# GpSimd instead of VectorE for the combination of the middle token tile's expert rows

## The chip, the cores and the metric

The kernel runs on one core of one Trainium2 chip. The metric is the device time of one execution in microseconds, the median over several runs. Times inside an execution are counted from the start of the profile's span.

## The reference, cut to what matters

One inference step of a two-layer backbone over 384 tokens of 1024 columns: 128 context tokens and 256 latent tokens. Each layer is a token mixer (HGRN2 in layer 0, a Fourier mixer in layer 1) and a hierarchical mixture of experts (16 experts, two chosen for a token), each with a gated residual; one norm closes the whole. The part at issue is the end of the mixture and what reads it:

```python
hid = jax.nn.silu(jnp.einsum('td,edf->tef', t, w_gate)) * jnp.einsum('td,edf->tef', t, w_up)
y = jnp.einsum('tef,te,efd->td', hid, gates.astype(hid.dtype), w_down)
...
x = x + g2[:, None, :] * _hier_moe(h, ...)      # end of a layer
...
h = _modulate(_rmsnorm(x, w['norm1_g'][i]), sh1, sc1)   # start of the next
...
return _rmsnorm(x, w['final_norm_g']), states
```

So for each token x + g2 * (w1 * y1 + w2 * y2) is wanted, where y1 and y2 are the rows that its two experts gave, w1 and w2 its weights and g2 the gate vector of its group.

## The kernel before, in words

All values are fp32. The tokens lie in three tiles of 128 (tile 0 is the context, tiles 1 and 2 the latent tokens), each a 128x1024 part of the tensor `x` in SBUF. The experts run as a loop (TensorE L755 for gate and up, L772 for down), their output rows are scattered to a buffer in HBM by GpSimd (L1340), and weights stream through a ring of six slots from SyncE's queue (`moe_units`, L334 to L349).

When the last rows of a layer are out, GpSimd sets `all_out`, and SyncE's `expert_rows` (L351 to L357) loads the rows back, one DMA for each tile, into `yall[:, t, 0]` and `yall[:, t, 1]`, the first and second expert's rows of the tile's tokens. Behind these it asks for the tables of the Fourier mixer and the next weights. Then

- ScalarE's `combine` (L932) multiplies the second rows of each tile by their weight in place (L937) and signals `second`;
- VectorE's `combine` (L1242) takes the tiles in order 0, 1, 2, three operations each, every one waiting for the one before: first rows times weight plus second rows (L1249), times the gate (L1251), added to x (L1252, signals `x_done`);
- ScalarE's `squares` (L814, the operation at L823) sums the squares of each tile, in order of the tiles, as its `x_done` comes;
- GpSimd's `rms` turns each sum into the factor 1/sqrt by two instructions on one column (L1410, L1413);
- after layer 0 VectorE's `normalise` (L992, the operation at L995) multiplies each tile by its factor, `columns` (L1001) prepares two vectors, and TensorE turns the tiles (L476): tiles 0 and 1 first, tile 2 behind. ScalarE (L831) and VectorE (L1016) bring the result back modulated, and TensorE begins the Fourier mixer (L658);
- after layer 1 VectorE's last loop (L1325) multiplies each tile by its factor and the final gain, and SyncE stores it (L424).

In every queue the order is that of the program text. On GpSimd, `rms("a1")` and `rms("fin")` stand right behind `experts(0)` and `experts(1)`. Between the two combinations lie the Fourier mixer, its output projection, the router (`route`) and layer 1's experts. The first six weight loads of layer 1 (L340) wait for a product of the modulation or of the projection, the later ones (L346, L349) for the experts' own progress.

Other lines that are named below: L1336, L1337 and L1346 are GpSimd's memsets at the start of its `experts`; L400 to L406 are the loads of the Fourier tables and weights, L332 those of the modulation's weights.

Of the kernel before, what the change touches and what calls it, by code (L numbers as in the profile page):

```python
# [25 lines left out]
ALU = mybir.AluOpType  # L26
# [5 lines left out]
TT = 3  # L32
# [40 lines left out]
def program(nc, io, scratch):  # L73
    with ExitStack() as ctx:
        def sb(name, shape, dt=F32):
            return ctx.enter_context(nc.sbuf_tensor(name, shape, dt))

        def sem(name):
            return ctx.enter_context(nc.semaphore(name))
# [3 lines left out]
        x = sb("x", [P, TT, D])  # L83
        hT = sb("hT", [P, KD, T])
        gate_bc = sb("gate_bc", [P, 2, 2, D])
# [11 lines left out]
        def c_(name):  # L97
            at, tile = (FIRST_AT, first) if name in FIRST_AT else (CONST_AT, const)
            a, b = at[name]
            return tile[:, a:b]  # L100
# [62 lines left out]
        yall = work[:, 0:2 * TT * D].rearrange("p (t c n) -> p t c n", t=TT, c=2)  # L163
# [5 lines left out]
        hid = me.take(F // 2).rearrange("p (j f) -> p j f", j=2)  # L169
        hidT = me.take(F // 2).rearrange("p (j s) -> p j s", j=2)  # L170
# [23 lines left out]
        wgt = sb("wgt", [P, 2, TT])  # L194
# [12 lines left out]
        gates_in = [sem(f"gates_in{i}") for i in range(4)]  # L207
# [27 lines left out]
        M = []  # L235
        for l in range(2):
            M.append({n: sem(f"moe{l}_{n}") for n in [
                "logits_t", "logits_sb", "logits", "chosen", "pos_mm", "onehots", "idx_mm", "idx_ready", "back_mm", "back_act",
                "hrow_out", "zeroed", "si_set", "gi_set", "gathered", "turned", "xt_sb", "gate_up_mm",
                "silu", "hid", "hid_turned", "hidT", "y_mm", "y_sb", "scattered", "gate_up_used", "used", "all_out", "second", "weights", "x_done",  # L240
                "exp_in", "exp_out"]})
        yback = [sem(f"expert_rows_in{t}") for t in range(TT)]
        chain = sem("dve_chain")
# [567 lines left out]
        def _(act):  # L811
            A = nc.scalar.activation

            def squares(name):  # L814

                for t in range(TT):
                    if name == "a0":
                        act.wait_ge(x_ready, 1)
                    elif name in ("m0", "m1"):
                        act.wait_ge(out_x[int(name[1])], 4 + t)  # L820
                    else:
                        act.wait_ge(M[0 if name == "a1" else 1]["x_done"], t + 1)
                    A(xn_of(name)[:, t, :], x[:, t, :], ACT.Square, accum_out=stat[:, t:t + 1]).then_inc(n_sq, 1)  # L823

            def modulate(name, l, which):
# [156 lines left out]
        def _(dve):  # L982
# [3 lines left out]
            def step(ins):  # L986

                count[0] += 1
                ins.then_inc(chain, 1)
                dve.wait_ge(chain, count[0])  # L990

            def normalise(name, tiles=range(TT)):  # L992
                for t in tiles:
                    dve.wait_ge(n_rs, 3 * NORM[name] + t + 1)
                    V.tensor_scalar(xn_of(name)[:, t, :], x[:, t, :], stat[:, 3 + t:4 + t], None, ALU.mult  # L995
                                    ).then_inc(n_xn, 1)
# [245 lines left out]
            def combine(l):  # L1242

                m = M[l]
                for t in range(TT):
                    dve.wait_ge(yback[t], 16 * (l + 1))
                    dve.wait_ge(m["second"], t + 1)
                    a, b = yall[:, t, 0, :], yall[:, t, 1, :]
                    step(V.scalar_tensor_tensor(out=a, in0=a, scalar=wgt[:, 0, t:t + 1], in1=b,  # L1249
                                                op0=ALU.mult, op1=ALU.add))  # L1250
                    step(V.tensor_tensor(a, a, gate_bc[:, 1, GROUP_OF[t], :], ALU.mult))  # L1251
                    V.tensor_tensor(x[:, t, :], x[:, t, :], a, ALU.add).then_inc(m["x_done"], 1)  # L1252
# [45 lines left out]
            experts(0)  # L1298
            dve.wait_ge(gates_in[1], 16 * 2)
            combine(0)  # L1300
            normalise("a1")
            dve.wait_ge(col_set, 10)
            columns("a1", 1, 0)
# [14 lines left out]
            experts(1)  # L1318
            dve.wait_ge(gates_in[3], 16 * 2)
            combine(1)  # L1320
            dve.wait_ge(M[1]["x_done"], TT)
            dve.wait_ge(fin_in, 16)
            for t in range(TT):
                dve.wait_ge(n_rs, 3 * NORM["fin"] + t + 1)
# [5 lines left out]
        def _(pool):  # L1330
            G_ = nc.gpsimd

            def experts(l):
# [68 lines left out]
                pool.wait_ge(m["xt_sb"], k1)  # L1402
                pool.sem_inc(m["all_out"], 1)

            def rms(name):

                for t in range(TT):
                    n = 3 * NORM[name] + t + 1
                    pool.wait_ge(n_sq, n)
                    G_.tensor_scalar(stat[:, t:t + 1], stat[:, t:t + 1], 1.0 / D, EPS, ALU.mult, ALU.add  # L1410
                                     ).then_inc(n_ms, 1)
                    pool.wait_ge(n_ms, n)
                    G_.tensor_tensor(stat[:, 3 + t:4 + t], stat[:, t:t + 1], c_("minus_half")[:, 0:1], ALU.pow  # L1413
                                     ).then_inc(n_rs, 1)
# [44 lines left out]
            pool.wait_ge(out_x[0], 6)  # L1459
            mod_gates(1, 0, gates_in[2])  # L1460
            experts(0)
            rms("a1")
            for U in (22, 23):
                gate_rows(U)
            rms("m1")
            mod_gates(1, 1, gates_in[3])
            experts(1)
            rms("fin")


# [107 lines left out]
```

## Time and profile before

| | us |
|---|---|
| median of 3 runs | 1196.88 |
| lowest, highest | 1189.55, 1198.07 |
| profiled execution | 1192.05 |
| its span | 1190.0 |
| TensorE busy | 985.6 (83%) |
| VectorE busy | 246.4 (21%) |
| GpSimd busy | 150.5 (13%) |
| mean granted TensorE clock | 0.917 of full speed |

In the profile PE is TensorE's matmul, PEld its weight load, DVE VectorE, ACT ScalarE, POOL GpSimd and SP SyncE; a name with q is the engine's queue. A row of the order of time gives start, length, engine, line, operation, output and inputs, shape and count, and in brackets how long the engine was idle before it and what ended that. The span goes from the first to the last instruction; 2.05 us of the profiled execution lie around it.

### The profile page before, as it was taken

The numbers are of one execution on the slowest core, as the hardware profiler recorded it, in microseconds if no ns is written. First come the engines' busy times: TensorE is split into PE (matmuls) and PEld (weight loads), VectorE is DVE, ScalarE is ACT, GpSimd is POOL, SyncE is SP. The second block draws the span as 40 slices with busy tenths as digits, with TensorE's granted clock in tenths as the row PEclk, the third lists the DMA queues.
The fourth block names the chain that finished last, engine by engine and source line by source line (L and its number), as shares of the span: only waits on it lengthen the run. The fifth ranks groups of instructions, "written<-read, shape, count | busy, mean of one in ns | idle before, by whom it ended". The sixth has DMA issues, their size and how long they took to land.

```text
span 1190.0 us, 21552 instructions
## 1 busy us (share of the span) xinstructions
PE 985.6 (83%) x8838; PEld 572.6 (48%) x8839; DVE 246.4 (21%) x546; ACT 229.0 (19%) x481; POOL 150.5 (13%) x249
## 2 busy tenths in 40 slices
PE   4799976999887895988898998299959998787770
PEld 3466545665456444544454554256445554444430
DVE  1100167100175144000000111500351010000004
ACT  1111102211102022211122222320131221121112
POOL 0000000100000120211111212100022221111112
PEclk9899989999987896988899999699978998998995
DMA  9966410777201741699989894815541999999943
GB/s 390 391 260 232 192 40 2 319 273 283 90 16 60 300 174 63 260 425 427 427 353 428 357 374 190 359 72 212 230 161 34 424 383 426 428 424 427 427 208 159
DMA packets 34184, 318.34 MB, mean 268 GB/s; under 512 B 6788, under 2 KB 9284, under 8 KB 16080
## 3 DMA queue, kind: packets, MB, share of 16 engines
q1 hardware_dynamic: 22016, 293.93, 59.9%
q0 software_dynamic: 8704, 18.33, 4.1%
q10 hardware_dynamic: 3408, 5.24, 1.2%
q8 instruction: 47, 0.77, 0.3%
q14 instruction: 9, 0.07, 0.0%
HBM read 309.12 MB, written 17.33 MB: 274 GB/s over the span
## 4 chain that ended last, share of the span: by engine, by line
PE 64%; DMA 23%; DVE 5%; issue 4%; ACT 2%; SPq 1%; POOLq 0%; POOL 0%; DVEq 0%; ACTq 0%
DMA ring<-in_moe_w_up 17%; PE ps L755 16%; PE ps L508 11%; PE ps L511 7%; PE ps L646 7%; PE ps L772 6%; PE ps L440 3%; DMA ring<-in_w_mod 2%; DMA work<-hrow,gi 2%; PE ps L548 2%; PE ps L658 2%; PE ps L718 1%; PE ps L675 1%; PE ps L487 1%; ACT hT L831 1%
## 5 line engine op out<-in xcount | busy, mean ns | idle before, releaser
L755 PE MATMUL ps<-ring,work 128*64 128x256 f32 x2432 | 304.0, 407 | 54.5 <-DMA ring<-in_moe_w_up 52.5
L755 PEld LDWEIGHTS ps<-ring,work 128*64 128x64 f32 x2432 | 187.4, 147 | 171.5 <-DMA ring<-in_moe_w_up 52.5
L772 PE MATMUL ps<-ring,work 128*64 128x512 f32 x608 | 145.3, 598 | 0.0
L508 PE MATMUL ps<-hT,ring 128*128 128x384 f32 x384 | 129.6, 496 | 5.2 <-ACT hT L831 5.2
L1235 DVE TENSOR_TENSOR work<-work,ps 128x128 f32<-128x128 f32 x76 | 21.8, 287 | 405.7 <-ACT work L924 405.7
L508 PEld LDWEIGHTS ps<-hT,ring 128*128 128x128 f32 x384 | 73.1, 193 | 56.2 <-ACT hT L831 5.3
L511 PE MATMUL ps<-ring,hT 128*128 128x512 f32 x192 | 91.6, 632 | 0.8 <-issue 0.8
L646 PE MATMUL ps<-ring,work 128*128 128x512 f32 x192 | 86.5, 611 | 1.3 <-ACT work L886 0.7
L772 PEld LDWEIGHTS ps<-ring,work 128*64 128x64 f32 x608 | 40.3, 136 | 55.3 <-issue 43.9
L440 PE MATMUL ps<-ring,scond 128*2 128x128 f32 x1536 | 48.0, 278 | 16.2 <-DMA ring<-in_w_mod 16.2
L646 PEld LDWEIGHTS ps<-ring,work 128*128 128x128 f32 x192 | 37.2, 196 | 48.3 <-issue 46.4
L511 PEld LDWEIGHTS ps<-ring,hT 128*128 128x128 f32 x192 | 37.5, 200 | 46.3 <-issue 45.9
L924 ACT ACT_TABLE_LOAD x38 | 48.8, 1283 | 51.4 <-issue 51.3
L1363 POOL COPY gi<-slots_idx 128x1 uint32 (+1 forms) x40 | 7.4, 185 | 392.5 <-issue 330.1
L440 PEld LDWEIGHTS ps<-ring,scond 128*2 128x2 f32 x1536 | 38.8, 86 | 27.9 <-issue 24.4
L926 ACT ACTIVATE work<-ps 128x128 f32<-128x128 f32 x76 | 21.1, 278 | 161.6 <-PE ps L751 97.4
L1340 POOL DMA_INDIRECT yrows<-work,si x44 | 45.1, 1026 | 53.7 <-POOL si L1373 35.1
L924 ACT ACTIVATE work<-ps 128x128 f32<-128x128 f32 x76 | 21.1, 278 | 157.3 <-PE ps L755 157.3
L1366 POOL DMA_INDIRECT work<-hrow,gi x40 | 42.2, 1056 | 33.8 <-POOL gi L1363 30.4
L1421 POOL DMA_DIRECT2D modrow<-mod_row x16 | 9.6, 602 | 277.4 <-DVE mod_row L1031 277.4
L1238 DVE COPY work<-ps 128x512 f32<-128x512 f32 x38 | 26.3, 692 | 70.0 <-PE ps L718 70.0
L929 ACT ACTIVATE work<-ps 128x512 f32<-128x512 f32 x38 | 22.7, 597 | 83.0 <-PE ps L772 70.6
(156 smaller groups left out, 771.3 us busy)
## 6 DMA issues: line engine op xcount, KB each, us to landing
ring<-in_moe_w_gate SPq DMA_DIRECT2D x32, 2048.0 KB, 13.2
ring<-in_moe_w_up SPq DMA_DIRECT2D x32, 2048.0 KB, 17.6
ring<-in_moe_w_down SPq DMA_DIRECT2D x32, 2048.0 KB, 21.7
ring<-in_w_mod SPq DMA_DIRECT2D x24, 2048.0 KB, 10.4
ring<-in_hgrn_w_in SPq DMA_DIRECT2D x10, 2048.0 KB, 11.9
work<-yrows SPq DMA_DIRECT2D x6, 1024.0 KB, 6.9
gate_bc<-modrow POOLq DMA_DIRECT2D x8, 512.0 KB, 6.0
ring<-in_hgrn_w_out SPq DMA_DIRECT2D x2, 2048.0 KB, 7.9
```

The source lines that it names most:

```text
L440: last = mm(ps[32 * c:32 * c + 2, bank, at:at + P], scond[:, :, k], slot3(s)[:, k, c * P:(c + 1) * P], start=(k == 0), stop=(k == KD - 1))
L508: last = mm(bank[:, 0:T], W[:, k, c * P:(c + 1) * P], hT[:, k, :], start=(k == 0), stop=(k == KD - 1))
L511: last = mm(bank, hT[:, k, c * P:(c + 1) * P], W[:, k, :], start=(k == 0), stop=(k == KD - 1))
L548: last = mm(bank[g * SMALL:(g + 1) * SMALL, o:o + SMALL], L[:, a:a + SMALL], R[:, a:a + SMALL], start=(j == 0), stop=(j == len(pairs) - 1))
L646: last = mm(ps[:, n % 4, :], src[:, k, t * P:(t + 1) * P], slot3(s)[:, k, :], start=(k == 0), stop=(k == KD - 1))
L658: last = mm(ps[:, 4 + n % 4, :], hT[:, 2 * g + k, t * P:(t + 1) * P], dft_c[:, k, :], start=(k == 0), stop=(k == 1))
L755: last = mm(ps[h * SLOTS:(h + 1) * SLOTS, GU_BANK[j], 0:2 * P], xt[:, k % 4, k // 4 * SLOTS:(k // 4 + 1) * SLOTS], Wgu[:, :, at:at + P], s ...
L772: last = mm(ps[h * SLOTS:(h + 1) * SLOTS, Y_BANK, :], hidT[:, j, q * SLOTS:(q + 1) * SLOTS], slot_d(S[2])[:, 2 * q + j, h * C512:(h + 1) * ...
L924: A(sg[:, j, :], ps[:, GU_BANK[j], 0:P], ACT.Silu).then_inc(m["silu"], 1)
L1238: V.tensor_copy(xt[:].rearrange("p k s -> p (k s)"), ps[:, XT_BANK, :]).then_inc(m["xt_sb"], 1)
L1340: G_.indirect_dma_start(out=scratch["y"][l], out_offset=bass.IndirectOffsetOnAxis(ap=si[:, 0:1], axis=0), in_=ysb, in_offset=None, bounds_ ...
L1366: G_.indirect_dma_start(out=xg, out_offset=None, in_=scratch["hrow"][l], in_offset=bass.IndirectOffsetOnAxis(ap=gi[:, 0:1], axis=0), bound ...
```

## The change

VectorE's `combine` goes over tiles 0 and 2 alone. A new `combine` on GpSimd, right behind its `experts` and ahead of its `rms`, does tile 1 in four instructions, each waiting for the one before. ScalarE's square of tile 1 waits for GpSimd's signal, and VectorE waits for it before it normalises (layer 0) or begins the final products (layer 1). ScalarE's own multiply of the second rows stays for all three tiles.

```diff
--- before.py
+++ after.py
@@ -237,7 +237,7 @@
             M.append({n: sem(f"moe{l}_{n}") for n in [
                 "logits_t", "logits_sb", "logits", "chosen", "pos_mm", "onehots", "idx_mm", "idx_ready", "back_mm", "back_act",
                 "hrow_out", "zeroed", "si_set", "gi_set", "gathered", "turned", "xt_sb", "gate_up_mm",
-                "silu", "hid", "hid_turned", "hidT", "y_mm", "y_sb", "scattered", "gate_up_used", "used", "all_out", "second", "weights", "x_done",
+                "silu", "hid", "hid_turned", "hidT", "y_mm", "y_sb", "scattered", "gate_up_used", "used", "all_out", "second", "weights", "x_done", "pool_sum", "pool_gated", "pool_x_done",
                 "exp_in", "exp_out"]})
         yback = [sem(f"expert_rows_in{t}") for t in range(TT)]
         chain = sem("dve_chain")
@@ -818,8 +818,10 @@
                         act.wait_ge(x_ready, 1)
                     elif name in ("m0", "m1"):
                         act.wait_ge(out_x[int(name[1])], 4 + t)
+                    elif t == 1:
+                        act.wait_ge(M[0 if name == "a1" else 1]["pool_x_done"], 1)
                     else:
-                        act.wait_ge(M[0 if name == "a1" else 1]["x_done"], t + 1)
+                        act.wait_ge(M[0 if name == "a1" else 1]["x_done"], t // 2 + 1)
                     A(xn_of(name)[:, t, :], x[:, t, :], ACT.Square, accum_out=stat[:, t:t + 1]).then_inc(n_sq, 1)
 
             def modulate(name, l, which):
@@ -1242,7 +1244,7 @@
             def combine(l):
 
                 m = M[l]
-                for t in range(TT):
+                for t in (0, 2):
                     dve.wait_ge(yback[t], 16 * (l + 1))
                     dve.wait_ge(m["second"], t + 1)
                     a, b = yall[:, t, 0, :], yall[:, t, 1, :]
@@ -1298,6 +1300,7 @@
             experts(0)
             dve.wait_ge(gates_in[1], 16 * 2)
             combine(0)
+            dve.wait_ge(M[0]["pool_x_done"], 1)
             normalise("a1")
             dve.wait_ge(col_set, 10)
             columns("a1", 1, 0)
@@ -1318,7 +1321,8 @@
             experts(1)
             dve.wait_ge(gates_in[3], 16 * 2)
             combine(1)
-            dve.wait_ge(M[1]["x_done"], TT)
+            dve.wait_ge(M[1]["x_done"], 2)
+            dve.wait_ge(M[1]["pool_x_done"], 1)
             dve.wait_ge(fin_in, 16)
             for t in range(TT):
                 dve.wait_ge(n_rs, 3 * NORM["fin"] + t + 1)
@@ -1402,6 +1406,22 @@
                 pool.wait_ge(m["xt_sb"], k1)
                 pool.sem_inc(m["all_out"], 1)
 
+            def combine(l):
+
+                m = M[l]
+                a, b = yall[:, 1, 0, :], yall[:, 1, 1, :]
+                pool.wait_ge(m["weights"], 1)
+                pool.wait_ge(yback[1], 16 * (l + 1))
+                G_.tensor_scalar(a, a, wgt[:, 0, 1:2], None, ALU.mult).then_inc(m["pool_sum"], 1)
+                pool.wait_ge(m["second"], 2)
+                pool.wait_ge(m["pool_sum"], 1)
+                G_.tensor_tensor(a, a, b, ALU.add).then_inc(m["pool_sum"], 1)
+                pool.wait_ge(gates_in[1 + 2 * l], 16 * 2)
+                pool.wait_ge(m["pool_sum"], 2)
+                G_.tensor_tensor(a, a, gate_bc[:, 1, 1, :], ALU.mult).then_inc(m["pool_gated"], 1)
+                pool.wait_ge(m["pool_gated"], 1)
+                G_.tensor_tensor(x[:, 1, :], x[:, 1, :], a, ALU.add).then_inc(m["pool_x_done"], 1)
+
             def rms(name):
 
                 for t in range(TT):
@@ -1459,12 +1479,14 @@
             pool.wait_ge(out_x[0], 6)
             mod_gates(1, 0, gates_in[2])
             experts(0)
+            combine(0)
             rms("a1")
             for U in (22, 23):
                 gate_rows(U)
             rms("m1")
             mod_gates(1, 1, gates_in[3])
             experts(1)
+            combine(1)
             rms("fin")
 
 
```

## Rows read from the trace of the kernel before

**Rows 1.** the page's busy table: busy us, share, instructions

```profile
PE 985.6 (83%) x8838; PEld 572.6 (48%) x8839; DVE 246.4 (21%) x546; ACT 229.0 (19%) x481; POOL 150.5 (13%) x249
```

**Rows 2.** the chain of waits, layer 0: start us, us, what

```profile
744.57 4.76 DMA work<-yrows
...
758.15 1.29 DVE work L1249
...
760.72 1.24 DVE x L1252
...
761.98 1.16 ACT work L823 x2
```

**Rows 3.** order of time, all engines, 750 to 765 us

```profile
750.72 1.28 DVE L1249 SCALAR_TENSOR_TENSOR work<-work,wgt 128x1024 f32<-128x1024 f32 x1 [11.35 <-ACT work L937]
751.92 1.15 ACT L937 ACTIVATE work<-work,wgt 128x1024 f32<-128x1024 f32 x1 [1.35 <-DMA work<-yrows]
...
755.02 1.15 ACT L937 ACTIVATE work<-work,wgt 128x1024 f32<-128x1024 f32 x1 [1.95 <-DMA work<-yrows]
...
758.37 1.50 POOL L1413 TENSOR_TENSOR stat<-stat,first 128x1 f32<-128x1 f32 x1
...
761.86 1.57 DVE L995 TENSOR_SCALAR work<-x,stat 128x1024 f32<-128x1024 f32 x2
...
763.58 4.71 PE L476 MATMUL ps<-first,work 128*128 128x128 f32 x24 [23.07 <-DVE work L995]
764.15 0.75 DVE L995 TENSOR_SCALAR work<-x,stat 128x1024 f32<-128x1024 f32 x1 [0.72 <-POOL stat L1413]
```

**Rows 4.** VectorE's three lines: ns min/median/max, starts

```profile
L1249 DVE SCALAR_TENSOR_TENSOR work<-work,wgt x6: 1276/1278/1283, 750.7 to 1173.5; 128x1024 f32<-128x1024 f32 x6
...
L1251 DVE TENSOR_TENSOR work<-work,gate_bc x6: 1224/1224/1226, 752.0 to 1174.8; 128x1024 f32<-128x1024 f32 x6
...
L1252 DVE TENSOR_TENSOR x<-x,work x6: 1224/1225/1226, 753.3 to 1176.1; 128x1024 f32<-128x1024 f32 x6
```

**Rows 5.** order of time, all engines, 1166 to 1181 us

```profile
1166.05 1.28 DVE L1249 SCALAR_TENSOR_TENSOR work<-work,wgt 128x1024 f32<-128x1024 f32 x1 [11.46 <-ACT work L937]
...
1177.31 2.48 DVE L1325 SCALAR_TENSOR_TENSOR work<-x,stat,gate_bc 128x1024 f32<-128x1024 f32 x2
...
1178.55 1.30 POOL L1410 TENSOR_SCALAR stat<-stat 128x1 f32<-128x1 f32 x1 [0.86 <-ACT work L823]
...
1180.51 1.28 DVE L1325 SCALAR_TENSOR_TENSOR work<-x,stat,gate_bc 128x1024 f32<-128x1024 f32 x1 [0.72 <-POOL stat L1413]
```

**Rows 6.** VectorE, then GpSimd, 441 to 443 us

```profile
441.70 1.79 DVE L995 TENSOR_SCALAR work<-x,stat 128x1024 f32<-128x1024 f32 x1
...
441.93 0.54 POOL L1336 MEMSET work<- 128x512 f32 x1
442.39 0.55 POOL L1337 MEMSET work<- 128x512 f32 x1
442.99 0.53 POOL L1346 MEMSET slots_idx<- 128x1 uint32 x1
```

**Rows 7.** GpSimd's two lines of rms: ns min/median/max, starts

```profile
L1410 POOL TENSOR_SCALAR stat<-stat x15: 183/192/1297, 13.9 to 1178.5; 128x1 f32<-128x1 f32 x15
...
L1413 POOL TENSOR_TENSOR stat<-stat,first x15: 550/556/1825, 14.2 to 1179.9; 128x1 f32<-128x1 f32 x15
```

**Rows 8.** SyncE's issues behind the expert rows

```profile
745.89 0.67 SPq L400 DMA_DIRECT2D work<-in_dft_c  x1
...
802.85 0.43 SPq L340 DMA_DIRECT2D ring<-in_moe_w_gate  x1
...
839.01 0.33 SPq L340 DMA_DIRECT2D ring<-in_moe_w_down  x1
```

**Rows 9.** stretches: busy us, PEclk, DMA share, GB/s

```profile
742.08:763.58 21.50, 0.00 (x1) 0.03 (x1) 12.44 (x11) 6.78 (x9) 6.37 (x7) 0.54 0.86 351
...
770.00:775.00 5.00, 4.99 (x12) 2.36 (x13) 0.00 (x0) 1.19 (x2) 0.00 (x0) 1.00 0.24 102
```

## The prediction

> **What bounds the kernel now.** I read the page's busy table first: TensorE is busy 83% of the span and VectorE 21% [rows 1], so VectorE's total is no bound; only its stretches on the chain of waits can cost. The chain of the work that ended last [rows 2] says which these are: behind each layer's expert loop it goes over the load of the expert rows, the three tiles' combination on VectorE (L1249, L1251, L1252), the tile squares on ScalarE and the small root on GpSimd, and TensorE stands still meanwhile (23.07 us, up to 763.58 [rows 3]). The change edits just this stretch, twice: after layer 0, where TensorE waits, and after layer 1, where the end of the program waits.
>
> The order of time in layer 0 is in [rows 3], the length of one VectorE operation in [rows 4]: 1.28, 1.22 and 1.22 us, and all six calls of each within 0.01 us. From 750.72 to 761.95 us VectorE runs the nine almost without a gap (9 operations of 1.24 us are 11.2), so the combination is VectorE-bound, not bound by the loads: tile 1's rows are there at 751.9 (ScalarE's L937 starts on them), tile 2's at 755.0. Layer 1 shows the same, 415.33 us later [rows 5].
>
> **What the change takes away.** Three VectorE operations a layer, 1.28 + 1.22 + 1.22 = 3.7 us. If that were all, tile 2 would be ready some 2 us earlier in layer 0: its second rows come from ScalarE at 755.02 + 1.15 = 756.2 [rows 3], and 3.7 us behind that is 759.9 against 761.95.
>
> **What it adds.** Four GpSimd operations over 128x1024 a layer: a multiply by the weight (one tensor input), and three with two tensor inputs (add, gate, add to x). No row has such an operation. The nearest: GpSimd's memset of 128x512 takes 0.54 us [rows 6], twice that is 1.09 us for one pass over 1024 columns; VectorE's own 1.22 us [rows 4]. The multiply: at least one pass, 1.09; at most two, 2.18 (read, then write). An operation of two inputs: at least one pass, 1.09; at most three, 3.27 (two reads and a write, one behind another). I take 1.09 for the multiply, which the one-input pass is nearest to, and 2.18 for the two-input ones, the two reads one after the other and the write beside them, halfway between the ends.
> The Trainium skill (GPSIMD Engine Reference, Elementwise — side-by-side cycle accounting) gives 4497 ns for an add over 2048 columns; an estimate by that page is 2.25 us for 1024, and the sum would be 0.4 us higher. No run here shows it yet.
>
> **The waits it adds.** GpSimd waits for tile 1's rows (there at 751.9), for ScalarE's weighted second rows (751.92 + 1.15 = 753.07) and for gates that were loaded long before; behind it in GpSimd's order stand the roots, for which VectorE's L995 waits. ScalarE's square of tile 1 waits for GpSimd's last sum, and tile 2's square stands behind it. VectorE waits for that sum ahead of all normalisation, columns and modulation. The renumbered waits of the squares ask for the same tile as before and cost nothing.
>
> **What lies beside what.** The decisive question is whether GpSimd's four run beside VectorE's six. The rows answer for one side. A one-element GpSimd instruction alone takes 0.19 us (L1410) or 0.55 us (L1413) [rows 7]; in the combination L1413 from 758.37 takes 1.50 [rows 3] and ends 0.44 us behind VectorE's L1249 (758.15 + 1.28 [rows 2]); L1410 at 1178.55 takes 1.30 and ends 0.06 us behind the second final product of VectorE (1177.31 + 2.48) [rows 5]. So a VectorE operation with two SBUF inputs holds GpSimd off until it ends. The other side: VectorE's normalisation (L995), 0.75 us in the combination [rows 3], takes 1.79 us beside GpSimd's two memsets, 1.04 more, which is about the two memsets' 1.09; and the one-element memset right behind takes 0.53, until L995 ends [rows 6]. So GpSimd holds VectorE off too, for one kind of operation. That VectorE's two-input operations were never stretched [rows 4] says little, as only one-element GpSimd instructions met them. I take it that they take turns in both directions.
> The Trainium skill (SBUF — State Buffer, SBUF: two separate sides) has a rule that speaks against the change and reaches further than the rows: a VectorE instruction with two SBUF inputs and a GpSimd instruction that reads SBUF exclude each other, the later one waiting until the other is done. By it the sum is the one below; by the unstretched rows alone it would be the third case below.
>
> **Layer 0, step by step.** With turns, VectorE and GpSimd alternate, each always waiting when the other ends: L1249 of tile 0 ends at 752.00 [rows 3]; multiply to 753.09; gate of tile 0 to 754.31; GpSimd's add to 756.49; x of tile 0 to 757.72; GpSimd's gate to 759.90; L1249 of tile 2 to 761.18; GpSimd's add to x to 763.36; gate of tile 2 to 764.58; x of tile 2 to 765.81. That is 3.86 us later than 761.95. In short: 1.09 + 3 x 2.18 = 7.63 added to one shared line, 3.7 removed.
> What is late next: the new work stands ahead of rms in GpSimd's order, and VectorE waits for pool_x_done before it normalises anything. Before, tiles 0 and 1 had their roots while VectorE was still combining, and L995 ran twice from 761.86. Now the root of tile 0 lands 0.45 behind x of tile 2, at 766.26; L995 of tile 0 (0.75) to 767.05; GpSimd's pair for tile 1 (0.19 + 0.55 and gaps, 0.9) to 767.95; L995 to 768.7, where TensorE can begin its turns (763.58 before); the pair for tile 2 to 769.6, where L995 of tile 2 starts, 5.4 us behind its 764.15. ScalarE's squares (1.16 us with their sum [rows 2], tile 1 behind 763.4, tile 2 behind 765.8) lie beside this and end at 767.0, in time for tile 2's pair. If the small pairs slip in beside L995, it is 3.9 instead of 5.4. I take 5.4.
> Nothing covers it. The DFT tables are asked for at 745.9 [rows 8], whatever the combination does, and the later loads (802.85, 839.01) wait for TensorE's own progress, so layer 1's weight stream moves with TensorE and the 5.4 us reach the end. TensorE's granted clock is 0.54 over the standstill and 1.00 from 770 [rows 9]; a standstill 5 us longer gives no reason for another level behind it, and I charge nothing.
>
> **Layer 1.** The same alternation from 1167.33 [rows 5] brings x of tile 2 to 1181.14 and the root of tile 0 to 1181.6. The final products (L1325, 1.28 us) then take turns with GpSimd's pairs: tile 0 to 1182.9, pair 1183.8, tile 1 to 1185.1, pair 1185.9, tile 2 starts at 1185.95, against 1180.51: 5.4 us. With the pairs beside the products it would be 3.7. What follows, the store and the end, is as before.
>
> **Sum.** 5.4 + 5.4 = 10.8 us. The profiled execution took 1192.05 us (span 1190.0), so the like of it would take 1202.9. The median of the runs shown is 4.8 higher, 1196.88, and the runs spread from 1189.55 to 1198.07; as the forecast is for a median I put it on that one: 1207.7 us, 0.9% slower. About 1% is what a measurement of this kernel can tell from no change, 12.0 us; the forecast is just inside.
>
> **The rivals.**
> 1. GpSimd is slower than I take it: three passes for two inputs and two for the multiply, turns as above. Each of four operations is 1.09 longer, twice: +8.7, so +19.5 us, 1216.4, slower by 1.6%. For it: three streams through an engine that shares its way with VectorE; against it: the memsets do a pass in 0.54 per 512. It decides from 2.38 us an operation on (1.2 us missing to 12.0, over six operations).
> 2. VectorE is not held off by GpSimd, while GpSimd still waits for it. VectorE ends at 759.95; GpSimd's multiply to 753.1, add to 755.4, gate to 757.7, and x, held off until gate 2 ends at 758.7, to 760.9. Squares, pairs and L995 then run to about where they did: +0.4 in layer 0, some -0.7 in layer 1: 1196.6. For it: [rows 4]; against it: [rows 6].
> 3. Nobody holds anybody off: GpSimd ends at 760.0, TensorE's wait ends 0.6 earlier, the last product 1.7 earlier: -2.3 us, 1194.6. Against it: [rows 3, 5].
> Even the best of these does not reach 1% faster: the squares and the roots of tiles 1 and 2 still have to follow tile 1's sum.
>
> **Chances.** Forecast 0.55, of which 0.15 lies over 12 us (operations of 2.4 us and more); rival 1, 0.22; rival 2, 0.12; rival 3, 0.08; others 0.03. Slower by over 1%: 0.15 + 0.22 = 0.37. Within: 0.40 + 0.20 less what the spread of runs takes, 0.59. Faster: 0.04, by that spread alone. The range goes from rival 2 on the median, 1196, to rival 1 just above it, 1217; the forecast's own is 1203 (the small pairs slip in, +7.6, on a somewhat lower median) to 1211.
>
> **What would show it.** In the profile after: four GpSimd operations of about 1.1 and 2.2 us with VectorE's of the same stretch stretched to 2.3 to 3.4 where they wait (or GpSimd's own stretched, as the profile may count waiting as work); x of tile 2 ending 15 us behind the first L1249 instead of 11.2; the first L995 only behind that; TensorE's idle time before its turns 28 us instead of 23.07. It is wrong if VectorE's six keep their 1.2 us and stand close together while GpSimd's large ones run, or if GpSimd's take over 2.4 us or near 1.2.

## The result, and the profile after

The changed kernel takes 1205.57 us (median of 8 runs, 1201.81 to 1209.64); the kernel before, run beside it, 1194.84 us (8 runs, 1189.55 to 1198.07). The ratio is 1.0104, with a 95% interval of 1.0083 to 1.0126: slower by about 1%, on the very bound up to which the prediction had counted as no change. The forecast was 1207.7 us in a range of 1196 to 1217.

The two profiled executions are 1190.0 and 1202.7 us of span. To see what the change did, each is cut at two marks of its stretch: ScalarE's first weighted rows (start), and tile 2's normalisation in layer 0 or its final product in layer 1 (start). Before: 764.15 - 749.42 = 14.73 us and 1180.51 - 1164.75 = 15.76 us. After, by the rows below and ScalarE's starts at 751.11 and 1171.85: 20.10 and 21.44. So the stretches cost 5.37 + 5.68 = 11.05 us. The rest of the 12.7 us is 1.69 that had come about before the first stretch, where nothing was changed, +0.04 between the two and -0.08 behind the second. That the part between comes out this even is in part luck: from one stretch to the next it takes 400.60 us before and 400.64 after, but 398.82 (e4_root_early) to 402.59 (e9_psum_multiply) in the other profiles whose experts do the same work, though no edit lies in it. The stretches are steadier: in the two profiles of one kernel (e5_tile0 and e5_again) they differ by 0.16 and 0.06 us. So the comparisons below go by them and not by the spans.

The order of time of the changed kernel in layer 0, ScalarE, VectorE and GpSimd; it answers to [rows 3]. L1251, L1253 and L1254 are VectorE's three operations, L1415, L1418, L1421 and L1423 GpSimd's four, L997 is the normalisation (of tile 2 in the row shown), L476 TensorE's turns:

```profile
751.11 1.15 ACT L939 ACTIVATE work<-work,wgt 128x1024 f32<-128x1024 f32 x1 [8.22 <-DMA work<-yrows]
752.40 1.28 DVE L1251 SCALAR_TENSOR_TENSOR work<-work,wgt 128x1024 f32<-128x1024 f32 x1 [11.39 <-ACT work L939]
...
753.71 3.89 POOL L1415 TENSOR_SCALAR work<-work,wgt 128x1024 f32<-128x1024 f32 x1 [8.98 <-DMA work<-yrows]
753.72 1.24 DVE L1253 TENSOR_TENSOR work<-work,gate_bc 128x1024 f32<-128x1024 f32 x1
754.99 1.94 DVE L1254 TENSOR_TENSOR x<-x,work 128x1024 f32<-128x1024 f32 x1
...
757.75 2.34 POOL L1418 TENSOR_TENSOR work<-work 128x1024 f32<-128x1024 f32 x1
...
758.01 3.17 DVE L1251 SCALAR_TENSOR_TENSOR work<-work,wgt 128x1024 f32<-128x1024 f32 x1 [1.07 <-ACT work L939]
...
760.24 3.14 POOL L1421 TENSOR_TENSOR work<-work,gate_bc 128x1024 f32<-128x1024 f32 x1
761.21 3.24 DVE L1253 TENSOR_TENSOR work<-work,gate_bc 128x1024 f32<-128x1024 f32 x1
763.45 3.20 POOL L1423 TENSOR_TENSOR x<-x,work 128x1024 f32<-128x1024 f32 x1
764.49 3.24 DVE L1254 TENSOR_TENSOR x<-x,work 128x1024 f32<-128x1024 f32 x1
...
770.64 4.18 PE L476 MATMUL ps<-first,work 128*128 128x128 f32 x24 [28.49 <-DVE work L997]
771.21 0.75 DVE L997 TENSOR_SCALAR work<-x,stat 128x1024 f32<-128x1024 f32 x1 [0.71 <-POOL stat L1433]
```

The reader is to subtract ends, not to read lengths, for a length here holds waiting. The multiply (L1415) stands from 753.71 but VectorE's gate of tile 0 runs its usual 1.24 to 754.96; then the sum into x of tile 0 starts at 754.99 and takes 1.94, 0.71 more than its 1.23: it was held off until 755.70. The add (L1418) runs from 757.75, and VectorE's L1251 of tile 2 takes 3.17 for its 1.28: it ends at 761.18, so it began to work at 759.90. GpSimd's gate (L1421) takes 3.14 and ends at 763.38, 2.20 behind 761.18. VectorE's gate (L1253) takes 3.24 and ends at 764.45, so it began at 763.22. From L1251 of tile 2 on, the two engines take turns without a gap: VectorE waits 2.15, 2.04 and 2.05 us, then works its 1.22 to 1.28. x of tile 2 is done at 767.73, 15.33 us behind the first L1251's start; before it was 11.23.

VectorE's three lines, which answer to [rows 4] (ns min/median/max):

```profile
L1251 DVE SCALAR_TENSOR_TENSOR work<-work,wgt x4: 1283/1284/3169, 752.4 to 1178.2; 128x1024 f32<-128x1024 f32 x4
...
L1253 DVE TENSOR_TENSOR work<-work,gate_bc x4: 1225/2240/3245, 753.7 to 1179.5; 128x1024 f32<-128x1024 f32 x4
...
L1254 DVE TENSOR_TENSOR x<-x,work x4: 1942/2631/3245, 755.0 to 1182.8; 128x1024 f32<-128x1024 f32 x4
```

Before, the largest of each was within 0.01 us of the smallest; now up to 2.02 us lie between them. The median hides this where only some of the calls meet GpSimd.

Layer 1, which answers to [rows 5]:

```profile
1174.65 3.77 POOL L1415 TENSOR_SCALAR work<-work,wgt 128x1024 f32<-128x1024 f32 x1 [9.35 <-DMA work<-yrows]
...
1178.19 1.28 DVE L1251 SCALAR_TENSOR_TENSOR work<-work,wgt 128x1024 f32<-128x1024 f32 x1 [0.44 <-ACT work L939]
1178.89 2.77 POOL L1418 TENSOR_TENSOR work<-work 128x1024 f32<-128x1024 f32 x1 [0.48 <-POOL work L1415]
...
1179.51 3.25 DVE L1253 TENSOR_TENSOR work<-work,gate_bc 128x1024 f32<-128x1024 f32 x1
...
1185.03 3.20 POOL L1423 TENSOR_TENSOR x<-x,work 128x1024 f32<-128x1024 f32 x1
...
1193.29 1.28 DVE L1329 SCALAR_TENSOR_TENSOR work<-x,stat,gate_bc 128x1024 f32<-128x1024 f32 x1 [0.72 <-POOL stat L1433]
```

Here L1251 of tile 2 got its turn before GpSimd's add, and GpSimd's last sum ends last, at 1188.23, 15.08 us behind the first L1251 (1173.15). In the chain of the page (its part 4) GpSimd, which had 0%, now has 3% of the span, the four operations of each layer and the roots behind them.

### The profile page after: what moved, and what is told of

The parts are those of the page before. It is cut to its first block, busy times and chain, and to the rows that moved or that the text cites. A ratio compares the mean times of both kernels' runs of the same rounds, so it can differ in the third digit from the quotient of the medians.

```text
span 1202.7 us, 21560 instructions
## 1 busy us (share of the span) xinstructions
PE 979.1 (81%) x8838; PEld 567.8 (47%) x8839; DVE 250.6 (21%) x540; ACT 228.7 (19%) x481; POOL 171.4 (14%) x257
## 4 chain that ended last, share of the span: by engine, by line
PE 61%; DMA 24%; issue 4%; DVE 4%; POOL 3%; ACT 2%; SPq 1%; POOLq 1%; DVEq 0%; ACTq 0%
DMA ring<-in_moe_w_up 18%; PE ps L755 15%; PE ps L508 11%; PE ps L511 7%; PE ps L646 7%; PE ps L772 5%; PE ps L440 3%; DMA work<-hrow,gi 3%; DMA ring<-in_w_mod 2%; PE ps L658 2%; PE ps L548 2%; PE ps L718 1%; DMA work<-yrows 1%; PE ps L675 1%; PE ps L487 1%
## 5 line engine op out<-in xcount | busy, mean ns | idle before, releaser
L755 PE MATMUL ps<-ring,work 128*64 128x256 f32 x2432 | 299.6, 402 | 60.5 <-DMA ring<-in_moe_w_up 58.5
```

What stands on the lines that cost most here:

```text
L755: last = mm(ps[h * SLOTS:(h + 1) * SLOTS, GU_BANK[j], 0:2 * P], xt[:, k % 4, k // 4 * SLOTS:(k // 4 + 1) * SLOTS], Wgu[:, :, at:at + P], s ...
```

## The experiments

Theory A: the two engines share a way into SBUF that a VectorE operation with two SBUF inputs and a GpSimd operation exclude each other from, so their times add. Rivals: they only share a bandwidth (B), any work beside the other costs (C), the order of GpSimd's queue is what costs (D), GpSimd's own chain of four bounds the stretch (E). All kernels start from the changed one unless said otherwise. The table gives the two stretches between the marks above and their sum against the 30.49 us of the kernel before, and the ratio of the times where the kernel was timed several times beside the one before. Where the ratio is missing the kernel was timed once (e1_serial 1210.55 us, e7_memsets 1179.84, e10_immediate 1196.81, e11_broadcast 1192.75), and its profile alone is used.

| kernel | layer 0 | layer 1 | against before | ratio, 95% interval |
|---|---|---|---|---|
| before | 14.73 | 15.76 | | |
| changed | 20.10 | 21.44 | +11.05 | 1.0104 (1.0083 to 1.0126) |
| e1_serial | 23.81 | 25.06 | +18.38 | |
| e2_psum | 16.83 | 18.36 | +4.70 | 1.0033 (1.0006 to 1.0059) |
| e3_psum_vector | 14.65 | 15.75 | -0.09 | 1.0008 (0.9976 to 1.0040) |
| e4_root_early | 21.08 | 21.20 | +11.79 | 1.0110 (1.0056 to 1.0164) |
| e5_tile0 | 13.72 | 14.48 | -2.29 | 0.9972 (0.9948 to 0.9996) |
| e5_again | 13.56 | 14.54 | -2.39 | 0.9985 (0.9959 to 1.0010) |
| e6_scalar_multiply | 18.44 | 19.52 | +7.47 | 1.0047 (1.0020 to 1.0075) |
| e7_memsets | 12.96 | 14.26 | -3.27 | |
| e9_psum_multiply | 15.98 | 17.10 | +2.59 | 1.0027 (1.0005 to 1.0050) |
| e10_immediate | 16.72 | 18.17 | +4.40 | |
| e11_broadcast | 15.94 | 17.22 | +2.67 | |

**e1_serial.** VectorE waits for GpSimd first:

```diff
             def combine(l):
                 m = M[l]
+                dve.wait_ge(m["pool_x_done"], 1)
                 for t in (0, 2):
```

> The changed kernel, but VectorE begins its tiles only when GpSimd's sum of tile 1 is done, so the two never meet. Theory A (they take turns on a shared way, in both directions): GpSimd's four alone take about 1.4 us (multiply) and 2.2 to 2.3 us (two inputs), as the changed kernel's unstretched rows and differences say, VectorE's six 1.22 to 1.28 us with none stretched; x of tile 2 ends some 2 us later in each layer than in the changed kernel (the serial sum plus the start 1.3 us later), the total is 2 to 5 us above the changed kernel's. Rival B (both run at once, each slowed by sharing a bandwidth): GpSimd's alone take well under 2 us (1.2 to 1.7), and the total is at or below the changed kernel's.

The order of time, layer 0 (L1416, L1419, L1422 and L1424 are GpSimd's four):

```profile
752.20 2.86 POOL L1416 TENSOR_SCALAR work<-work,wgt 128x1024 f32<-128x1024 f32 x1 [8.94 <-DMA work<-yrows]
...
755.20 2.34 POOL L1419 TENSOR_TENSOR work<-work 128x1024 f32<-128x1024 f32 x1
757.69 2.34 POOL L1422 TENSOR_TENSOR work<-work,gate_bc 128x1024 f32<-128x1024 f32 x1
760.11 2.34 POOL L1424 TENSOR_TENSOR x<-x,work 128x1024 f32<-128x1024 f32 x1
762.55 1.28 DVE L1252 SCALAR_TENSOR_TENSOR work<-work,wgt 128x1024 f32<-128x1024 f32 x1 [23.00 <-POOL x L1424]
```

Alone, each two-input operation takes 2.34 us, and VectorE's take 1.22 to 1.28 again. Rival B is out: it wanted GpSimd's well under 2 us and a total at or below the changed kernel's. But the multiply takes 2.86 us where 1.4 was expected. That figure had been read out of the changed kernel's rows, as 0.74 (754.96 to 755.70) and 0.67 (756.93 to 757.60) on the shared way. Only the first of these is the way held: the multiply ends 2.64 us after VectorE's gate at 754.96, no more than its 2.86 alone, although VectorE ran 1.23 us in between, so for the rest of its time it doesn't exclude VectorE. The stretches became 3.71 and 3.62 us longer than in the changed kernel, not 2, and 7.33 together where 2 to 5 were expected; of the 1.7 or so that each is over, the longer multiply accounts for 1.46.

**e2_psum.** No VectorE operation of the combination has two inputs in SBUF. First ScalarE's edit (the `and True` has no effect), then VectorE's:

```diff
-                    A(yall[:, t, 1, :], yall[:, t, 1, :], ACT.Copy, scale=wgt[:, 1, t:t + 1]
+                    b = yall[:, t, 1, :] if t == 1 and True else ps[:, 2 * t:2 * t + 2, :].rearrange("p b n -> p (b n)")
+                    A(b, yall[:, t, 1, :], ACT.Copy, scale=wgt[:, 1, t:t + 1]
...
-                    a, b = yall[:, t, 0, :], yall[:, t, 1, :]
-                    step(V.scalar_tensor_tensor(out=a, in0=a, scalar=wgt[:, 0, t:t + 1], in1=b,
+                    a, b = yall[:, t, 0, :], ps[:, 2 * t:2 * t + 2, :].rearrange("p b n -> p (b n)")
+                    step(V.scalar_tensor_tensor(out=b, in0=a, scalar=wgt[:, 0, t:t + 1], in1=b,
...
-                    step(V.tensor_tensor(a, a, gate_bc[:, 1, GROUP_OF[t], :], ALU.mult))
-                    V.tensor_tensor(x[:, t, :], x[:, t, :], a, ALU.add).then_inc(m["x_done"], 1)
+                    step(V.tensor_tensor(b, b, gate_bc[:, 1, GROUP_OF[t], :], ALU.mult))
+                    V.tensor_tensor(x[:, t, :], x[:, t, :], b, ALU.add).then_inc(m["x_done"], 1)
```

> The changed kernel, but ScalarE puts the weighted second rows of tiles 0 and 2 into PSUM, and VectorE keeps its sum there, so that none of its six operations has two inputs in SBUF. Theory A (only VectorE operations with two SBUF inputs exclude GpSimd's reads): VectorE's six take 1.2 to 1.3 us each, GpSimd's four 1.4 and 2.3 us, beside each other; x of tile 2 ends 9.3 us behind the first L1251 start and GpSimd's sum 10.1 us behind it; the first matrix turn comes about where it does in the kernel before; ratio to before 0.998 to 1.002. Rival C (any work of one engine slows the other): rows stretched to 3.2 us as in the changed kernel, ratio 1.008 to 1.012.

The order of time, layer 0:

```profile
752.41 1.23 DVE L1254 TENSOR_TENSOR ps<-ps,gate_bc 128x1024 f32<-128x1024 f32 x1
752.42 2.86 POOL L1416 TENSOR_SCALAR work<-work,wgt 128x1024 f32<-128x1024 f32 x1 [8.91 <-DMA work<-yrows]
...
755.42 2.35 POOL L1419 TENSOR_TENSOR work<-work 128x1024 f32<-128x1024 f32 x1
...
756.19 1.29 DVE L1252 SCALAR_TENSOR_TENSOR ps<-work,wgt,ps 128x1024 f32<-128x1024 f32 x1 [1.29 <-ACT ps L940]
...
757.51 1.23 DVE L1254 TENSOR_TENSOR ps<-ps,gate_bc 128x1024 f32<-128x1024 f32 x1
757.91 2.35 POOL L1422 TENSOR_TENSOR work<-work,gate_bc 128x1024 f32<-128x1024 f32 x1
758.78 1.22 DVE L1255 TENSOR_TENSOR x<-x,ps 128x1024 f32<-128x1024 f32 x1
760.34 2.34 POOL L1424 TENSOR_TENSOR x<-x,work 128x1024 f32<-128x1024 f32 x1
```

The same operations on the same engines at the same time, and nothing is stretched: VectorE's 1.22 to 1.29, GpSimd's 2.34 to 2.35. Rival C is out, and the turns are shown to come from VectorE's second SBUF input. (Its first two operations now also write to PSUM; but the sum into x, L1255, writes to SBUF as before, differs in the second input alone, and is not stretched either.) The turns cost 11.05 - 4.70 = 6.35 us of the stretches. Two things missed: the ratio, 1.0033, is above the expected 1.002, though its interval reaches down to 1.0006; and TensorE's first turn comes 16.27 us behind ScalarE's start, not 14.16 as in the kernel before. GpSimd is the bound here, and its multiply takes 2.86 us, not 1.4: its sum ends 12.86 us behind ScalarE's start (749.82), where 11.4 would follow from 1.4.

**e3_psum_vector.** The control: the kernel before, all three tiles on VectorE, in this form of the operands.

```diff
-                    a, b = yall[:, t, 0, :], yall[:, t, 1, :]
+                    a, b = yall[:, t, 0, :], ps[:, 2 * t:2 * t + 2, :].rearrange("p b n -> p (b n)")
...
```

> The kernel before (all three tiles on VectorE) with the weighted second rows and the sum in PSUM: the control for the form of the operands alone. Theory A: 1.2 to 1.3 us an operation as before, ratio 0.998 to 1.002. If PSUM operands are dearer, each of nine operations shows it (0.1 us more would be 1.8 us in all).

Ratio 1.0008, stretches within 0.1 us of before. The form costs nothing by itself and gains nothing. It takes the waits from GpSimd's side too: the roots of tiles 0 and 1, which had taken up to 1.82 us beside the combination, take 0.19 and 0.55 to 0.57 here, but they were not the bound.

**e4_root_early.** Tile 0's root goes ahead of GpSimd's last addition, and VectorE takes tile 0 before it waits.

```diff
+                rms("a1" if l == 0 else "fin", [0])
                 pool.wait_ge(m["pool_gated"], 1)
                 G_.tensor_tensor(x[:, 1, :], x[:, 1, :], a, ALU.add).then_inc(m["pool_x_done"], 1)
...
+            normalise("a1", [0])
             dve.wait_ge(M[0]["pool_x_done"], 1)
-            normalise("a1")
+            normalise("a1", [1, 2])
...
+                if t == 1:
+                    dve.wait_ge(M[1]["pool_x_done"], 1)
```

> The changed kernel, but GpSimd's root of tile 0 stands ahead of its last addition and VectorE normalises (or finishes) tile 0 before it waits for GpSimd's sum. Theory A: of the 5.4 us a layer, 3.9 to 4.1 us come from the turns and the rest from roots and normalisations that all stand behind the last sum; this takes 0.3 to 0.6 us in layer 0 and about 1 us in layer 1: 1 to 2 us below the changed kernel, ratio to before 1.007 to 1.009. Rival D (most of the loss is the order of the queue, not the turns): 4 us and more below the changed kernel, ratio under 1.006.

Both missed: instead of 1 to 2 us less it is 0.98 us more in layer 0 and 0.24 less in layer 1. The order of time in layer 0 says why (L1433 is the first of the root's two, L1426 is the addition):

```profile
762.79 3.24 DVE L1254 TENSOR_TENSOR x<-x,work 128x1024 f32<-128x1024 f32 x1
765.04 1.05 POOL L1433 TENSOR_SCALAR stat<-stat 128x1 f32<-128x1 f32 x1
...
766.73 2.33 POOL L1426 TENSOR_TENSOR x<-x,work 128x1024 f32<-128x1024 f32 x1
766.78 2.84 DVE L997 TENSOR_SCALAR work<-x,stat 128x1024 f32<-128x1024 f32 x1 [0.74 <-POOL stat L1436]
...
772.73 0.75 DVE L997 TENSOR_SCALAR work<-x,stat 128x1024 f32<-128x1024 f32 x1 [0.71 <-POOL stat L1436]
```

The root's pair (765.04 to 766.73) stands in front of the addition while VectorE goes through with its last sum to 766.03; so the addition has nothing left to overlap with, and now the normalisation of tile 0 (L997, a one-input operation) is held off by it too, 2.84 us for 0.75. Rival D, that the order of the queue makes most of the loss, is out in this form. That the roots all follow the last sum does cost (in the changed kernel's layer 0 the last sum ends 4.10 us later, the normalisation of tile 2 starts 5.37 later), but not in a way that this exchange could win back.

**e6_scalar_multiply.** ScalarE weighs tile 1's first rows, GpSimd keeps three operations.

```diff
+                    if t == 1:
+                        A(yall[:, t, 0, :], yall[:, t, 0, :], ACT.Copy, scale=wgt[:, 0, t:t + 1]
+                          ).then_inc(M[l]["first"], 1)
...
-                G_.tensor_scalar(a, a, wgt[:, 0, 1:2], None, ALU.mult).then_inc(m["pool_sum"], 1)
...
+                pool.wait_ge(m["first"], 1)
```

> The changed kernel, but ScalarE multiplies tile 1's first rows (1.15 us, between its own second rows) in place of GpSimd's multiply, which alone took 2.86 us but held VectorE off for only 0.7. Theory A: the multiply's own time lay mostly beside VectorE's work, so the path loses only the 0.7 us that it held the shared way, and less where ScalarE's extra operation delays tile 2's second rows: 0.3 to 1 us a layer, total 0.5 to 2 us below the changed kernel. Rival E (GpSimd's chain of four, 2.86 + 3 x 2.34, is what bounds the stretch, turns or not): 1.7 us and more a layer, total 3.5 us and more below.

Measured: 3.58 us less in the stretches, ratio 1.0047. A's 0.5 to 2 us is missed, and E's "3.5 and more" is met. In the changed kernel of layer 0 the multiply cost the 0.71 us that it held VectorE off and then 0.82 us in which the way stood idle (756.93 to 757.75), since the multiply was still at work and VectorE waited for tile 2's second rows; 1.53 of the 1.66 us won. So a chain of GpSimd's own stands beside the turns. It is not all, as E would have it: here the turns are still there,

```profile
755.46 3.14 POOL L1421 TENSOR_TENSOR work<-work,gate_bc 128x1024 f32<-128x1024 f32 x1
...
756.44 3.25 DVE L1256 TENSOR_TENSOR work<-work,gate_bc 128x1024 f32<-128x1024 f32 x1
758.68 3.20 POOL L1423 TENSOR_TENSOR x<-x,work 128x1024 f32<-128x1024 f32 x1
759.72 3.24 DVE L1257 TENSOR_TENSOR x<-x,work 128x1024 f32<-128x1024 f32 x1
```

and the next run takes them away.

**e9_psum_multiply.** The edits of e2_psum and e6_scalar_multiply together.

> e2_psum with ScalarE's multiply for tile 1: no operation of VectorE has two SBUF inputs, and GpSimd's chain is three operations of 2.34 us in place of 2.86 + 3 x 2.34. Theory A: here GpSimd's chain bounds the stretch, so the saving goes straight to the path: GpSimd's sum ends 11.7 us behind ScalarE's first start in place of 12.9, 1 to 1.3 us a layer, ratio to before 1.000 to 1.003, some 2.5 us below e2_psum. If instead VectorE is the bound there, no difference from e2_psum.

Ratio 1.0027, stretches 2.11 us below e2_psum. Against e6_scalar_multiply the turns alone are 7.47 - 2.59 = 4.88 us. Theory A's 1 to 1.3 us a layer is met in layer 1 (1.26) and just missed in layer 0 (0.85), by no more than the two profiles of e5_tile0's kernel differ, and GpSimd's sum ends 11.99 us behind ScalarE's start, 11.7 expected; the ratios of the two kernels cannot be told apart by themselves.

**e7_memsets.** Each of GpSimd's four is a memset of the same size, the first now behind ScalarE's weighted rows as well; tile 1's expert rows are left out of the result, so layer 1 has other rows to work on and only the stretches are compared.

```diff
-                G_.tensor_scalar(a, a, wgt[:, 0, 1:2], None, ALU.mult).then_inc(m["pool_sum"], 1)
+                G_.memset(a, 0.0).then_inc(m["pool_sum"], 1)
...
-                G_.tensor_tensor(x[:, 1, :], x[:, 1, :], a, ALU.add).then_inc(m["pool_x_done"], 1)
+                G_.memset(a, 0.0).then_inc(m["pool_x_done"], 1)
```

> The changed kernel with each of GpSimd's four operations replaced by a memset of the same 128x1024 (tile 1's expert rows are left out of the result): it writes, but reads nothing. Theory A with reads alone in conflict: VectorE's L1251, L1253 and L1254 take 1.22 to 1.28 us each, unstretched, beside memsets of about 1 us. Theory A with any GpSimd access in conflict: VectorE's operations that meet a memset are stretched by about 1 us each, the memsets too.

```profile
756.20 0.95 POOL L1416 MEMSET work<- 128x1024 f32 x1 [10.08 <-ACT work L939]
756.31 1.23 DVE L1254 TENSOR_TENSOR x<-x,work 128x1024 f32<-128x1024 f32 x1
757.21 0.95 POOL L1418 MEMSET work<- 128x1024 f32 x1
...
759.03 1.28 DVE L1251 SCALAR_TENSOR_TENSOR work<-work,wgt 128x1024 f32<-128x1024 f32 x1 [1.49 <-ACT work L939]
759.22 0.95 POOL L1422 MEMSET work<- 128x1024 f32 x1
```

VectorE's sum into x from 756.31 takes its 1.23 beside two memsets, and they take 0.95 each. So it is GpSimd's reads that meet VectorE's second input. Before, L995 had been stretched by a memset [rows 6]: that one-input operation runs 1024 columns in 0.75 us where the two-input ones need 1.22, and is another case.

**e10_immediate and e11_broadcast.** Why the multiply takes 2.86 us, both from e2_psum; in the first, tile 1's first rows stay unweighted. The first added line is e10_immediate's, the second e11_broadcast's.

```diff
-                G_.tensor_scalar(a, a, wgt[:, 0, 1:2], None, ALU.mult).then_inc(m["pool_sum"], 1)
+                G_.tensor_scalar(a, a, 1.0, None, ALU.mult).then_inc(m["pool_sum"], 1)
+                G_.tensor_tensor(a, a, wgt[:, 0, 1:2].to_broadcast((P, D)), ALU.mult).then_inc(m["pool_sum"], 1)
```

> e2_psum with GpSimd's multiply by the constant 1.0 in place of the weight of each partition (tile 1's first rows stay unweighted). Theory F (the 2.86 us of the multiply come from fetching the weight from SBUF for each partition): the multiply takes about 1 us, as the memset's 0.95. Theory G (they belong to this operation on GpSimd whatever the scalar is): 2.8 us again. By F the stretch from ScalarE's first start to tile 2's normalisation is 1.5 to 1.8 us shorter than in e2_psum (16.8), by G the same.

> e2_psum with GpSimd's multiply written as an operation of two tensors, the weight repeated along the row (a step of zero). Theory F: two reads, 2.34 us as its other two-input operations, 0.5 us less than in e2_psum a layer. Theory G: 2.34 us too; this run alone doesn't tell F from G, but says whether the other form is the cheaper one.

GpSimd's multiply of layer 0 in e10_immediate:

```profile
753.37 2.80 POOL L1416 TENSOR_SCALAR work<-work 128x1024 f32<-128x1024 f32 x1 [8.86 <-DMA work<-yrows]
```

and in e11_broadcast:

```profile
750.23 1.89 POOL L1416 TENSOR_TENSOR work<-work,wgt 128x1024 f32<-128x1024 f32 x1 [8.92 <-DMA work<-yrows]
```

2.80 us with a constant: theory G, it belongs to the operation, not to the fetching of the weight, and the stretches stay within 0.3 us of e2_psum's. Written with two tensors the same multiply takes 1.89 us, less than the 2.34 that both theories had expected, and e11_broadcast's stretches are 2.03 us shorter than e2_psum's.

**e5_tile0 and e5_again.** The version that the theory suggests, run twice: the operands as in e2_psum; GpSimd takes tile 0, whose rows land first; ScalarE weighs its first rows; squares, roots and normalisations go 1, 0, 2. The last two pieces are from VectorE's and from GpSimd's combination:

```diff
+        def order_of(name):
+            return (1, 0, 2) if name in ("a1", "fin") else (0, 1, 2)
...
-                for t in (0, 2):
+                for t in (1, 2):
...
-                a, b = yall[:, 1, 0, :], yall[:, 1, 1, :]
+                a, b = yall[:, 0, 0, :], yall[:, 0, 1, :]
...
+                pool.wait_ge(m["first"], 1)
```

> The version that theory A suggests: as e2_psum, but GpSimd takes tile 0, whose rows land 2.4 us before tile 1's and 5.1 before tile 2's, ScalarE multiplies its first rows (1.15 us in place of GpSimd's 2.86), and squares, roots and normalisations go in the order 1, 0, 2. Theory A: GpSimd's three two-input operations of 2.34 us end 9.7 us behind ScalarE's first start, VectorE's six, unstretched, 11.2 us behind it (12.5 in the kernel before), the normalisation of tile 2 starts 13.4 us behind it (14.7 before): 1.3 us a layer won, ratio to before 0.996 to 0.999. Rival C (any meeting of the two engines costs): above 1.002.

> e5_tile0 once more, since its interval reached 0.9996. If its gain is that of the stretches in its profile (1.0 us in layer 0 and 1.3 in layer 1, 2.3 of 1192), the ratio is 0.998 and the interval of this run holds it; if it was luck, the ratio lies at 1.000 or above.

The order of time of e5_tile0 in layer 0 (L1427, L1430 and L1432 are GpSimd's, L1262 is VectorE's sum into x):

```profile
745.72 2.34 POOL L1427 TENSOR_TENSOR work<-work 128x1024 f32<-128x1024 f32 x1 [8.68 <-ACT work L947]
...
748.20 2.35 POOL L1430 TENSOR_TENSOR work<-work,gate_bc 128x1024 f32<-128x1024 f32 x1
...
750.63 2.36 POOL L1432 TENSOR_TENSOR x<-x,work 128x1024 f32<-128x1024 f32 x1
...
753.61 1.22 DVE L1262 TENSOR_TENSOR x<-x,ps 128x1024 f32<-128x1024 f32 x1
...
757.10 0.75 DVE L1005 TENSOR_SCALAR work<-x,stat 128x1024 f32<-128x1024 f32 x1 [0.72 <-POOL stat L1442]
```

GpSimd ends at 752.99, 9.61 us behind ScalarE's start (743.38; 9.7 expected), VectorE at 754.83, 11.45 behind it (11.2 expected, 12.53 in the kernel before). Of the 1.3 us expected a layer, 1.01 and 1.28 came, in e5_again 1.17 and 1.22. e9_psum_multiply has the same operands and the same three operations of GpSimd; the other tile and the other order take 2.59 + 2.29 = 4.88 us off it (the two were not tried apart). Both profiles show 2.3 to 2.4 us less in the stretches than before, the ratios are 0.9972 and 0.9985, and the second interval holds 1. So the gain is shown in the profiles and is about what can be timed at all.

## Why the prediction was right

**What bounds the stretch: right.** The combination lay on the path in both layers, and what is behind it moved: -0.08 us behind the second stretch, and +0.04 between the two, where the profiles agree to no better than 2 us or so.

**Turns in both directions: right, with a correction.** The prediction took this from [rows 3, 5 and 6] against the unstretched [rows 4]; that choice was the decisive one. e2_psum shows it, at 6.35 us of the 11.05. The memsets of [rows 6] were a poor witness for it, though: e7_memsets shows that what only writes doesn't hold off a two-input operation. The Trainium skill (SBUF — State Buffer, SBUF: two separate sides) says that such a VectorE instruction excludes a GpSimd one that reads SBUF; the changed kernel, e2_psum and e7_memsets agree on each half of the sentence. Where it says that the shared way is held for the whole instruction, the multiply differs: it held VectorE off for 0.71 of its 2.86 us, and the measurement decides.

**The two-input operations: right.** 2.18 us were taken, from two passes of a memset; alone they take 2.34, and in turns they hold VectorE off for 2.04 to 2.15. That it came this near is in part luck: the pass of 1.09 us was twice a memset of 512 columns, where one of 1024 takes 0.95 (e7_memsets), and no run shows that an operation of two inputs is made of two such passes.
The estimate of 2.25 us from the figure of the Trainium skill (GPSIMD Engine Reference, Elementwise — side-by-side cycle accounting) for twice the columns lies between; the trace of e1_serial has 2.34, and the measurement decides.

**The multiply: its size was wrong.** 1.09 us were taken, with 2.18 as the upper end; it takes 2.86 alone, and by the prediction's own sign (over 2.4 us) this term was wrong. It came out nearly even by chance: as a hold it is 0.71 us instead of 1.09, and 0.82 us of idle way came in, which no step had. e6_scalar_multiply prices the whole of it at 3.58 us over both layers.

**The order of the turns: partly wrong.** GpSimd's add was to go between VectorE's gate and sum of tile 0, 3.59 us behind the start of the first L1249; it came 5.35 behind, after that sum, as the multiply was still at work. In layer 1 it came one turn later still, so that GpSimd's sum, not VectorE's, ended last. The total hardly changes, for on a way that is never idle the holds add up to the same in any order.

**The sum.** In layer 0, x of tile 2 was to end 15.09 us behind the first L1249 and ended 15.33 behind it; in layer 1 it is GpSimd's sum that ends 15.08 behind. What is late next, roots and normalisations one behind another, was to make 5.4 us of 3.86; measured 5.37 of 4.10, and TensorE's idle time before its turns is 28.49 us as against the 28 named. The final products of layer 1 were to be 5.4 later, measured 5.68. Together 10.8 forecast, 11.05 in the profile, and 10.73 between the medians. The forecast median, 1207.7, is 2.1 above the measured one because it was put on the median of three runs, 1196.88, where the eight runs beside the changed kernel have 1194.84.

**The rivals.** Rival 1 was out, if narrowly: 2.34 us is below the 2.38 from which it was to decide, and far from its own 3.27; for the multiply even its 2.18 was too low. Rivals 2 and 3 needed VectorE's operations unstretched; e2_psum, which makes them so, still costs 4.7 us against the -0.3 and -2.3 named: 2.11 of it is the multiply (e9_psum_multiply), and the other 2.59 lies in GpSimd's three operations of 2.34 us, which end last there, and in the squares and roots behind them; how these two share it wasn't tried.

**The bound of 1%.** With 1.0083 to 1.0126 the measurement doesn't say on which side of 1% the change lies; 0.59 for within and 0.37 for slower left that open.

## What to carry to other kernels

Before elementwise work is moved from VectorE to GpSimd, count VectorE's operations with two SBUF inputs in the same stretch: against GpSimd operations that read SBUF their times add (here 1.2 and 2.1 us in turn), unless one of the inputs is put into PSUM, which was free here. Give GpSimd the tile whose data come first (with the order of the roots to match, 4.88 us here), and keep single-input scaling on ScalarE (1.13 to 1.15 us here against 2.86). A stretched length with a normal median is found by the maximum of a line, and what an operation costs by the differences of ends.

## What the hardware showed that was not expected

GpSimd's multiply of one tensor by a scalar over 128x1024 takes 2.86 us with a weight from SBUF and 2.80 with a constant, more than an add of two tensors (2.34) and than the same multiply with the weight repeated as a second tensor (1.89); a memset of that size takes 0.95. Why the one-input form is the dearest stays open.

The first block behind the standstill, 48 matmuls of the Fourier mixer (L658 or L661), takes 20.85 us in some profiles and 22.55 in others. Three stretches of the changed kernel (the first column is the length, the next TensorE's busy time; the granted clock stands third from the end):

```profile
770.64:776.00 5.36, 4.18 (x24) 3.94 (x24) 4.30 (x14) 3.72 (x11) 0.54 (x1) 0.74 0.36 153
776.70:779.50 2.80, 2.77 (x4) 1.25 (x5) 0.00 (x0) 0.00 (x0) 0.00 (x0) 0.53 0.00 0
...
782.00:790.00 8.00, 8.00 (x20) 3.55 (x19) 0.00 (x0) 2.98 (x5) 0.00 (x0) 1.00 0.01 2
```

In its 22.55 us the block begins near the lower level (0.53 of 2.4 GHz is about 1.2 GHz) and rises to the full 2.4 GHz, where the kernel before has 1.00 from 770 on [rows 9] and 20.85 us. It doesn't go by the length of the standstill: 20.85 also behind 29.4 us (e4_root_early) and 22.55 behind 21.9 (e5_again). What goes with it is the turns just before: 4.1 to 4.4 us there with 22.55, 4.7 to 5.4 with 20.85. Kernels with GpSimd's combination are found on both sides. Why the clock has fallen again at the block's start in the one case and not in the other stays open, and whether one kernel varies in it from run to run isn't shown (the only one profiled twice, e5_tile0's, has 22.55 both times). The block lies between the two stretches, so a reader who compares two spans here has to set its 1.7 us aside.
